# Prompt attention by head pairs in two parts, turned three steps behind the scores

## The reference

```
s_c = einsum('btgjd,bcgd->btgjc', qg, kc) - slopes * c_dist      # 63 compressed keys
p_c = masked_softmax(s_c, c_mask);  o_c = einsum('btgjc,bcgd->btgjd', p_c, vc)
...  # "selected": with 16 blocks of 64 and 1024 positions, all keys up to the query
p_s = masked_softmax(s_s, s_dist >= 0);  o_s = einsum('btgjm,btgmd->btgjd', p_s, v_g)
s_w = einsum('btgjd,blgd->btgjl', qg, kw) - slopes * w_dist      # window of 512 keys back
p_w = masked_softmax(s_w, w_mask);  o_w = einsum('btgjl,blgd->btgjd', p_w, vw)
o = g[:, :, 0] * o_c + g[:, :, 1] * o_s + g[:, :, 2] * o_w
```

## Time and profile before

| | before |
|---|---|
| runs, median (lowest to highest) | 1683.64 us (1683.38 to 1683.86) |
| the profiled execution's own time | 1680.46 us |
| its span | 1678.7 us |
| PE busy over the span | 1624.0 us (97%) |
| DVE, ACT, POOL busy | 854.6, 576.9, 396.6 us |
| mean granted TensorE clock | 0.996 |
| the stage, first score matmul to last value matmul | 668.4 to 912.3 us |

### The profile page before, as it was taken

The page is one execution under the profiler, slowest core; times in us unless marked ns, Lnnn a source line. Parts: engine busy times, 40 slices in busy tenths (PEclk is TensorE's granted clock), DMA queues, the critical chain, the costliest instruction groups (busy, mean ns, idle before and its releaser), DMA issues. The chain is left out here.

```text
span 1678.7 us, 45635 instructions
## 1 busy us (share of the span) xinstructions
PE 1624.0 (97%) x20051; PEld 1163.1 (69%) x20051; DVE 854.6 (51%) x1790; ACT 576.9 (34%) x1244; POOL 396.6 (24%) x455
## 2 busy tenths in 40 slices
PE   8999999999999999999999999999999999999997
PEld 6788777777777555676767889766578888445443
DVE  3433456556555354776776664541152465624344
ACT  5221344454533213666663111223312211102444
POOL 0212223333331130556444220223100032000120
PEclk9999999999999999999999999999999999999999
DMA  5112000100101314712001976468611420700001
GB/s 168 38 50 57 3 17 17 29 17 16 29 17 35 89 32 101 231 74 86 18 2 62 309 286 208 144 144 193 156 26 25 142 60 1 277 0 1 26 25 50
DMA packets 111450, 136.81 MB, mean 82 GB/s; under 512 B 42940, under 2 KB 93829, under 8 KB 106046
## 3 DMA queue, kind: packets, MB, share of 16 engines
q1 hardware_dynamic: 102002, 84.61, 17.3%
q0 software_dynamic: 9216, 49.29, 9.4%
q10 hardware_dynamic: 36, 0.01, 0.0%
HBM read 121.28 MB, written 17.15 MB: 82 GB/s over the span
## 5 line engine op out<-in xcount | busy, mean ns | idle before, releaser
L1265 PE MATMUL ps<-xnT,rw_side_w 64*64 64x344 f32 x2304 | 219.3, 459 | 1.6 <-issue 0.9
L1265 PEld LDWEIGHTS ps<-xnT,rw_side_w 64*64 64x64 f32 x2304 | 98.1, 135 | 33.6 <-issue 12.9
L2733 PE MATMUL ps<-xnT,zT 128*128 128x344 f32 x384 | 120.1, 457 | 0.0
L2447 POOL TENSOR_SCALAR probs<-probs,row_sums,gates 128x63 f32<-128x63 f32 (+6 forms) x148 | 95.6, 662 | 94.8 <-DVE row_sums L2403 94.3
L2733 PEld LDWEIGHTS ps<-xnT,zT 128*128 128x128 f32 x384 | 69.5, 190 | 33.1 <-issue 3.4
L2352 ACT ACTIVATE probs<-probs,neg_max 128x63 f32<-128x63 f32 (+6 forms) x148 | 87.5, 595 | 0.0
L2325 PE MATMUL ps<-probsT,kvtok 128*64 128x128 f32 x1056 | 75.3, 280 | 0.0
L2298 PE MATMUL ps<-kT,zT 64*128 64x512 f32 (+3 forms) x384 | 72.0, 485 | 2.5 <-DVE neg_max L2393 1.6
L2368 ACT ACTIVATE probsT<-ps 128x512 f32<-128x512 f32 (+1 forms) x80 | 45.9, 574 | 82.3 <-PE ps L2311 82.3
L3443 POOL TENSOR_TENSOR mT<-mT,gate_n 128x258 f32<-128x258 f32 x28 | 23.7, 854 | 211.7 <-DVE gate_n L3406 211.7
L2311 PE MATMUL ps<-ident,probs 128*128 128x128 f32 (+1 forms) x460 | 68.1, 279 | 4.8 <-DVE probsT L2424 3.2
(11 more groups left out here) (625 smaller groups left out, 3584.5 us busy)
## 6 DMA issues: line engine op xcount, KB each, us to landing
w_z<-in_w_in_dram SPq DMA_DIRECT2D x13, 512.0 KB, 5.0
xnT_kept<-xnT SPq DMA_DIRECT2D x1, 4128.0 KB
x_tok<-in_x_prompt_dram SPq DMA_DIRECT2D x8, 512.0 KB
rw_side_w<-in_w_in_dram SPq DMA_DIRECT2D x16, 256.0 KB, 3.3
zT<-in_w_in_dram SPq DMA_DIRECT2D x8, 512.0 KB
ring_k<-in_w_in_dram SPq DMA_DIRECT2D x8, 512.0 KB, 5.3
w_out<-in_w_out_dram SPq DMA_DIRECT2D x1, 4096.0 KB
h_tok<-in_x_prompt_dram SPq DMA_DIRECT2D x8, 512.0 KB, 8.3
```

Source lines behind the costliest of these rows:

```text
L1265: last = nc.tensor.matmul(k.ps[half(f), bank, 0:CG], w.side[half(e), g // 3 % 2, c, half(f)], k.xnT[half(e), c, third(g)], start=(phase == ...
L2447: nc.gpsimd.tensor_scalar(every, every, ls[:, at:at + 1], k.gates[:, i, gate:gate + 1], ALU.mult, ALU.mult).then_inc(scaled, 1)
L2733: ins = self.nc.tensor.matmul(self.k.ps[:, self.banks[n % nb], 0:CG], self.w[:, t % 2, c, :], self.k.xnT[:, c, g * CG:(g + 1) * CG], start ...
```

## The change

A unit, now w, is a pair of heads (j and j+1) with one query tile, so there are 16. It is cut into two parts, the selected branch first, then window and compressed, and each part has its own coefficients, its own scaling and its own entry in the queue: 32 groups of 4 or 8 POOL instructions. There are 80 score steps. A piece is one key tile for both heads and both groups, again four transposes; there are 148 pieces where there were 160. The value matmul takes both heads as one moving block of 256 columns. The lead goes from 4 steps to 3, the queue gives four pieces at most, the tile order becomes 0, 3, 7, 1, 6, 2, 5, 4, the ring grows from 6912 to 8400 columns, and its places are searched instead of run through in turn. POOL's four DMAs stay halfway through (unit 8 of 16).

```diff
-AT_RING, AT_LEAD, AT_GROUP, AT_SLOTS = 6912, 4, 4, 5
-AT_ORDER = (0, 4, 7, 1, 6, 2, 5, 3)
+AT_RING, AT_LEAD, AT_GROUP, AT_SLOTS = 8400, 3, 4, 5
+AT_ORDER = (0, 3, 7, 1, 6, 2, 5, 4)
 AT_SHORT_FIRST = (4, 5, 6)
+AT_PARTS = ((1,), (2, 0))
...
+        self.N = 2 * NT
+        self.steps, self.last_step = [], {}
+        for w in range(self.N):
+            i = self.tile(w)
+            for part, branches in enumerate(AT_PARTS):
+                full, rest = [], []
+                for q in range(2):
+                    for br in branches:
+                        width = self.width(w, br)
+                        cuts = list(range(0, width, 512))
+                        short_first = i in AT_SHORT_FIRST and len(cuts) == 2
+                        for lo in cuts:
+                            n = min(512, width - lo)
+                            first, final = (n < 512, n == 512) if short_first else (lo == 0, lo + 512 >= width)
+                            (full if n == 512 else rest).append((w, q, br, lo, n, first, final))
+                packed = []
+                for piece in rest:
+                    for s in packed:
+                        if sum(p[4] for p in s) + piece[4] <= 512:
+                            s.append(piece)
+                            break
+                    else:
+                        packed.append([piece])
+                self.steps += packed + [[p] for p in full] if i in AT_SHORT_FIRST else [[p] for p in full] + packed
+                self.last_step[w, part] = len(self.steps) - 1
+
...
+        self.groups = [(w, part) for w in range(self.N) for part in range(2)]
+        self.pieces, self.group_pieces, self.last_of, self.last_piece, self.first_piece = [], {}, {}, [], []
+        for w, part in self.groups:
+            if part == 0:
+                self.first_piece.append(len(self.pieces))
+            start = len(self.pieces)
+            for br in AT_PARTS[part]:
+                self.pieces += [(w, br, t) for t in range(self.tiles(w, br))]
+                self.last_of[w, br] = len(self.pieces) - 1
+            self.group_pieces[w, part] = list(range(start, len(self.pieces)))
+            if part == 1:
+                self.last_piece.append(len(self.pieces) - 1)
...
-        while ready < self.N and self.last_step[ready] + AT_LEAD <= s:
-            queue = queue + list(range(self.first_of[ready], self.last_piece[ready] + 1))
+        while ready < len(self.groups) and self.last_step[self.groups[ready]] + AT_LEAD <= s:
+            queue = queue + self.group_pieces[self.groups[ready]]
             ready += 1
-        now = queue[:AT_GROUP + (len(queue) > 8)]
+        now = queue[:AT_GROUP]
         for a in range(0, max(len(waiting), len(now)), 2):
...
-EARLY_CHUNKS = 16
+EARLY_CHUNKS = 8
...
             def turn(pc):
-                n = plan.pieces[pc][0][0]
-                pe.wait_ge(scaled, 6 * n + max(2 * (3, 1, 2)[br] for _, br, t in plan.pieces[pc]))
+                w, br, t = plan.pieces[pc]
+                m = NCMP if br == 0 else P
+                pe.wait_ge(scaled, scaled_at[w, br])
                 if pc >= 2:
                     pe.wait_ge(pt_v if pc % 2 else pt_a, (pc - 2) // 2 + 1)
-                for b, (n, br, t) in enumerate(plan.pieces[pc]):
-                    m = NCMP if br == 0 else P
-                    for g in range(2):
-                        last = nc.tensor.transpose(k.ps[0:m, 4 + pc % 2, (2 * b + g) * P:(2 * b + g + 1) * P],
-                                                   region(n, br, g, t * P, m), k.ident[:])
+                for g in range(2):
+                    for q in range(2):
+                        last = nc.tensor.transpose(k.ps[0:m, 4 + pc % 2, (2 * g + q) * P:(2 * g + q + 1) * P],
+                                                   region(w, q, br, g, t * P, m), k.ident[:])
                 last.then_inc(pt_ps, 1)
 
             def values(pc):
-                n = plan.pieces[pc][0][0]
-                if pc == plan.first_of[n] and n >= 2:
-                    pe.wait_ge(gatedo, n - 1)
+                w, br, t = plan.pieces[pc]
+                m = NCMP if br == 0 else P
+                if pc == plan.first_piece[w] and w >= 2:
+                    pe.wait_ge(gatedo, w - 1)
                 pe.wait_ge(pt_v if pc % 2 else pt_a, pc // 2 + 1)
-                for b, (n, br, t) in enumerate(plan.pieces[pc]):
-                    m = NCMP if br == 0 else P
-                    for g in range(2):
-                        at = (1 + 2 * br) * P + g * HD
-                        vals = k.vc[:, half(g)] if br == 0 else k.kvtok[:, plan.first_tile(n, br) + t, at:at + HD]
-                        last = nc.tensor.matmul(k.ps[half(g), 6 + n % 2, 0:P], vals,
-                                                pt[0:m, pc % NPT, (2 * b + g) * P:(2 * b + g + 1) * P],
-                                                start=(br == 1 and t == 0), stop=(br == 0))
+                for g in range(2):
+                    at = (1 + 2 * br) * P + g * HD
+                    vals = k.vc[:, half(g)] if br == 0 else k.kvtok[:, plan.first_tile(w, br) + t, at:at + HD]
+                    last = nc.tensor.matmul(k.ps[half(g), 6 + w % 2, 0:2 * P], vals, pt[0:m, pc % NPT, 2 * g * P:2 * (g + 1) * P],
+                                            start=(br == 1 and t == 0), stop=(br == 0))
                 last.then_inc(pvd, 1)
 
             for kind, u in plan.events:
...
+            def coefs(e):
+                w, part = plan.groups[e]
+                c = slice(column(w, 0, AT_PARTS[part][0], 0), column(w, 1, AT_PARTS[part][-1], 1) + 1)
+                dve.wait_ge(expd, exped_at[w, part])
+                nc.vector.tensor_scalar(ls[:, c], ls[:, c], 1e-30, None, ALU.max).then_inc(capped, 1)
+                dve.wait_ge(capped, e + 1)
+                nc.vector.reciprocal(ls[:, c], ls[:, c]).then_inc(coef, 1)
...
-                    while done < plan.N and plan.last_step[done] + 2 <= u:
+                    while done < len(plan.groups) and plan.last_step[plan.groups[done]] + 2 <= u:
                         coefs(done)
                         done += 1
...
+            for e, (w, part) in enumerate(plan.groups):
+                j, i = plan.head(w), plan.tile(w)
+                if (w, part) == (EARLY_CHUNKS, 0):
                     pool.wait_ge(xn_out, 16)
                     for m in range(4):
...
+                pool.wait_ge(coef, e + 1)
+                for br in AT_PARTS[part]:
+                    for q in range(2):
+                        for g in range(2):
+                            at, gate = column(w, q, br, g), 8 * br + 4 * g + j + q
+                            every = region(w, q, br, g, 0, plan.width(w, br))
+                            nc.gpsimd.tensor_scalar(every, every, ls[:, at:at + 1], k.gates[:, i, gate:gate + 1], ALU.mult,
+                                                    ALU.mult).then_inc(scaled, 1)
 
```

More of the change, by code:

```diff
@@ L2151, in __init__ @@
             queue, waiting, ready = self.turns(s + 1, queue, waiting, ready)
-        while ready < self.N or queue or waiting:
+        while ready < len(self.groups) or queue or waiting:
             self.events.append(("R", len(self.events)))
             queue, waiting, ready = self.turns(len(self.steps) + AT_LEAD, queue, waiting, ready)
[L2156 to L2159, removed]
-                for g in range(2):
[L2161 to L2170, removed]
@@ L2171, in __init__ @@
-        where = {e: p for p, e in enumerate(self.events)}
-        for (n, br, g), m in self.freed.items():
-            first = min(s for s, parts in enumerate(self.steps) for part in parts if part[0] == n and part[1] == br)
-            assert m is None or where["T", self.last_piece[m]] < where["S", first], (n, br, g, m)
+        where = {e: p for p, e in enumerate(self.events)}
+        self.place, self.freed, taken = {}, {}, []
+        for w in range(self.N):
+            for br in (1, 2, 0):
+                for q in range(2):
+                    first = where["S", self.first_step(w, q, br)]
+                    last = self.last_of[w, br]
+                    for g in range(2):
+                        n = self.width(w, br)
+                        held = [h for h in taken if where["T", h[2]] >= first]
+                        at = min(self.room(n, held), key=lambda a: (self.newest(a, n, taken), a))
+                        over = [h[2] for h in taken if h[0] < at + n and at < h[1]]
+                        self.place[w, q, br, g] = at
+                        self.freed[w, q, br, g] = max(over) if over else None
+                        taken = [h for h in taken if not (h[0] < at + n and at < h[1])] + [(at, at + n, last)]
@@ L2252, in attend_prompt, with region, column @@
         masked_at, count = {}, 0
[L2253 to L2255 removed]
+        masked_step, exped_at, exps_done = [], {}, 0
+        for s, parts in enumerate(plan.steps):
+            for w, q, br, lo, n, first, final in parts:
```

(31 more changed lines are left out.)

97 lines of the change are left out of this document (50 added, 47 removed).

## The result

The changed kernel takes 1729.0 us (median of four, 1727.6 to 1730.0) against 1683.5, a ratio of 1.027 (95% interval 1.025 to 1.029): 45 us slower. The profiled execution took 1728.2 us, its span 1726.5. The stage lasts from 667.9 to 961.7 us, 293.8 us.

The account below looks back on a forecast made before the run. PE's own work was taken to bound the stage. Waits rising from 13 to 50.9 us (+37.9), less 5.7 of PE work, gave +32.2; with 4 for the clock and 3.2 to the median, 1720 us, range 1702 to 1736.

Parts of the forecast that it names:

- What bounds, and the chain: PE's work sets the end; turns wait for masks, coefficients and four scalings after even last steps, 35.0 us in sum.
- Start: Stage start: turns of tile 7 come about 39.3 us after the first score, 15.0 waited, 6.4 not already listed.
- End: Last group, tile 4's window part: exponentials, coefficients and four scalings take 8.9 us against 4.5 of PE work; 4.4 us wait.
- The four DMAs: POOL's DMAs halfway through the stage: the following tile 3 is scaled 1.1 us late.
- PE's work: PE's matmuls in the stage: wider value matmuls and fewer changes of matmul kind, together 5.7 us less.
- The part of the width: Value matmuls on PE: 148 blocks of 256 columns replace 296 of 128; 2.0 us less, bounds nothing to 3.0.
- The clock: Clock falls at PE's long waits: one or two taken, 4 us; bounds no fall to about nine falls, 31 us.
- the second rival: The clock falls at most of the long waits, adding 22 to 31 us in place of 4, near 1740; chance 13%.
- PE busy time that grew: Sign of being wrong, through clock or matmul prices; the forecast had PE busy 5 us less in the stage.
- The first: Rival: turns find their scaling done, so only saved matmul time and some small waits count, 1673 us; chance 4%.
- The third: Rival: half of the waiting is absent because other engines catch up while PE is stopped, 1703 us; chance 14%.
- The fourth: Rival: value matmul width hardly matters, a 256-column block costs as one of 128, 1690 us; chance 2%.

Follow-up runs that it names:

- scaling experiment: Changed kernel with POOL scaling only the first 128 columns of each block of probabilities, the rest left unscaled: 1694.5 us, ratio 1.009.
- the first experiment: Changed kernel with transposes of the identity put on PE ahead of each group's first turn that waits for scaling: 1712.9 us, ratio 1.021.

## Why the prediction was right

- **What bounds, and the chain.** Right. The waits forecast and measured (PE idle, first and second run) are: tile 7 5.5 and 4.9, measured 5.1 and 4.5; tile 6 4.4 twice, measured 4.6 twice; tile 5 3.5, measured 3.3 and 3.35; tile 4 1.5, measured 1.45 both times; tile 3's window part 3.1 and 2.7, measured 3.1 and 2.4. That is 33.9 us for 35.0. The scaling experiment moved them by four scalings, the tile order moved them to other tiles, and with lead 4 PE's waits on POOL were 3.6 us in all. PE's idle time in the stage grew by 35.9 us, for 37.9.
- **Start.** The turns of tile 7 began 708.5 - 667.9 = 40.6 us into the stage (39.3 forecast), but by another sum: PE idled 11.4 us of it and not 15.0, and the clock stood at half for 8.9 us of it. The sum is near in part by luck.
- **End.** From the turn of tile 4's selected part to the first turn of its window part 9.0 us passed (943.24 to 952.24) for 8.9, with 4.1 us waited for 4.4, in two pieces of 2.15 and 1.93. The first piece is named after POOL but follows a copy on DVE (948.86 to 949.54), which stood behind 3.6 us of waiting for exponentials; with the short scalings it stayed 2.15, while the second went.
- **The four DMAs.** 1.1 us on tile 3. Measured 0.6 before its selected part, and 0.9 before the window part of tile 0; neither wait is there in the first run. No run took the DMAs away, so their part is not shown.
- **PE's work.** 5.7 us less forecast. The kernel with lead 4 and ring 8700, without clock falls in the stage, has 6.9 less busy, but its order has 193 changes of kind where the changed kernel has 205 and the kernel before 230. The part of the width was mis-sized: 2.0 us forecast, but two 256-column record pairs start 0.216 us apart, 0.432 a block where two of 128 need 0.436, so 0.6 us. The other 6.3 us over 37 changes of kind are 0.17 each, for 0.15; by that the changed kernel saves about 4.9 us, an estimate.
- **The clock.** The term that was mis-sized: 4 us for one or two falls, where there were ten. The kernel with PE kept busy puts it at 14.5 us of the stage. No run shows the price of one fall on which the 4 us rest, and the second rival's 22 to 31; the runs showed these 14.5 us for ten stretches at half clock against one. The stage grew by 50.6 us for 36.2; 10.5 of these 14.4 us are the clock. Without the clock the forecast was 32.2 us more, and the filled stage is 36.1 longer. The second rival, clock falls at most long waits, was the right picture of how often, and its price of 22 to 31 us too high: half of 47.8 us would be 23.9, but PE idled in 5.5 us of it, and six of the ten stretches were 3.4 us and not 6.8; what makes up the rest of the difference to 14.5 is not shown. The prediction also named PE busy time that grew as a sign of being wrong. It grew, by 15 us, and the cause was the clock: PE's own work is 229.5 us in the filled kernel.
- **The number.** 1720 was forecast within 1702 to 1736; 1729 is in it. The stage alone missed by more, 14 us. In the profiled execution the rest of the program was 2.8 us shorter, and the median lies 0.8 us above that execution where the forecast added 3.2, so part of the miss was covered by chance.
- **The other rivals.** The first needed turns that find their scaling done, and PE waits about 41 us for scaling. The third (half of the waits gone because the other engines catch up) is refuted by the list above. The fourth is refuted by the kernel with value matmuls of 128 columns.

## What to carry to other kernels

When work is placed by step numbers and steps come in pairs, a lead of n steps is two different leads; write down for each unit what the waiting engine still has to do between the event that starts its chain and the wait, and compare it with the chain's sum. A tile order can be worth more than a wider matmul: two swapped tiles (with a larger ring) were 27 us, 256 columns in place of 128 nothing that could be measured. And look at the granted clock around TensorE's long waits: it was halved within or behind 20 of the 21 above 3 us in the stage of these traces, and here ten falls were 14.5 us beside 36 of longer waits. Filling the waits with idle transposes told the two apart: half clock in the stage went from 47.8 to 3.4 us.

## What was not expected of the hardware

The clock fell behind or within 20 of the 21 waits above 3 us in the stage of these traces; the one without a fall is the 3.1 us wait of the kernel with lead 4 and ring 8700. But it fell for 3.4 us in some and 6.8 in others (once 10.2, with the tile order of before), and not for as long at the same wait in each kernel: the changed kernel had ten stretches of half clock in the stage, 47.8 us, the same kernel with narrow value matmuls nine, 44.4 us in all. Behind waits of at most 2.4 us it fell in some cases and not in others: with the short scalings four times, with lead 4 and the ring of 8400 columns twice (6.8 us), in the kernel before never in the stage. What decides it in a single case stays open. PE kept its full clock while it did nothing but transposes of the identity for 3.9 us at a time (1.00 from 737.5 to 741.4 in the first experiment).
